# A two-block fp32 model on one core: the order of an attention, of a norm, of two PSUM banks and of a gate group changed, and three short products put into one block

## The chip, the cores and the metric

One core of one Trainium2 chip. The time is the device time of one execution in microseconds (us); times of several executions are given as their median. TensorE is called PE here (its weight loads PEld), VectorE DVE, ScalarE ACT, GpSimd POOL, SyncE SP.

## The reference, cut to what matters

The model takes 256 tokens of 1024 features through two blocks. The first has a gated short convolution, a SwiGLU feed-forward, a latent attention with 8 heads and a second SwiGLU. The second has one wide projection, a chunked band attention beside an mLSTM, a gated mix of both, and a PEER layer that chooses 16 of 16384 experts for each of 8 heads. All is float32.

```python
h = h + mla_mixer(rms_norm(h, mla_norm_g), w_dq, q_norm_g, w_uq, w_o, k_nope, k_pe, v, cos, sin)
h = h + swiglu_ffn(rms_norm(h, mla_ffn_norm_g), w13, w2)
x = rms_norm(h, final_norm_g)
h = modulate(rmsnorm(x, norm1_g), sh1, sc1)            # the "mix" norm
qa, ka, va, qkb, vb, ob, ib, fb, ga, gb = split(h @ w_in)
...
s = einsum("thpd,hpnd->thpn", q, sub_keys); s_top, i_top = top_k(s, 16)   # "the choice"
act = gelu(einsum("thkd,td->thk", u_exp[e], xb))       # here: for all experts, then gated
y = einsum("thk,thkd->td", gate * act, v_exp[e])
```

## The kernel before, in words

The kernel streams 525 blocks of weights, 128 x 1024 float32 each, through a ring of three buffers. SP loads block n into `raw` as soon as the low part of block n-3 is made. ACT rounds it to `wh` (`ahead`, line 1183, called `hi` below), DVE subtracts to get the rest `wl` (line 1736, called `lo`), and PE makes of each fp32 product three products, high x high, low x high, high x low (`three`, lines 552 to 554). A block is 24 such products of 256 columns. `hi` and `lo` run two blocks ahead of PE (LEAD = 2), and each stands at a place in the engine's program that was written by hand among that engine's other work. Each engine runs its program in order.

What the change touches, in the order of time:

- **Start.** POOL loads the condition row `cond_row`, ACT applies Silu to it (line 1277) in between the first convolution tiles, then `hi` of the next blocks.
- **Latent attention.** For each head PE makes scores (line 798), transposes probabilities (811), mixes values (820) and projects (`out_of_head`). DVE masks (2123), divides (2130, 2131), subtracts (2168), makes `lo` and a piece of the condition's product (`ada_piece`, 1905).
- **The norm "mix"** after the second feed-forward. DVE adds the eight result tiles to `h` (2003), with one `lo` after the second; ACT squares all eight tiles (1201); PE sums them over partitions (614); ACT takes the root (1215); DVE inverts and scales; ACT and DVE split into high and low parts (1225, 1779).
- **The projection** `proj(k)`, 45 blocks. Results go to the PSUM tensor `wk` of four banks; blocks 9 to 12 (vb) and 13 to 16 (va) both write banks 0 and 1 with 512 columns. ACT copies them out (1519). Beside them runs the mLSTM, unit by unit, with short PE products, DVE `m_weigh` (2303 to 2313) and ACT exponentials.
- **The choice.** `early(i)` makes the activations of 128 expert rows i; ACT writes them out (1626, 1644). During the first 77 of these blocks DVE finds the 16 best of each head and token; its `lo` calls stand there where a planner's estimated costs (`PER_LO` = 1616 per call) put them. After block 66 ACT takes an exponential (1657).
- **Gates.** Then DVE makes one-hot matrices (2552, 2556) for four tokens at a time, PE multiplies them (`gate_group`, 1092), ACT copies the result out (1631). 64 groups go with 48 further blocks, three blocks (`u_block`) to four groups; the first such trip is written out.
- `shift_phase` (line 567, 569) puts three short fp32 products, whose result nobody reads, between the products of one block: 128 columns after the second feature group, 256 after the fourth, 128 after the sixth. The kernel has it in the third block of both feed-forwards, in block 2 and block 79 of the experts' first pass and in the third block of their second pass.

The semaphores that the steps speak of: `lo_ready` (PE waits for a block's low part), `conv_kept` and `proj_act` (ACT has read a result), `probs`, `masked`, `mixed_lo` (DVE's results for the attention), `hot_ready` and `hot_used` (one-hot matrices made and used).

Of the kernel before, what the change touches and what calls it, by code (L numbers as in the profile page):

```python
# [24 lines left out]
ALU = mybir.AluOpType  # L25
# [7 lines left out]
P = 128  # L33
# [111 lines left out]
MIX_FILL = 8  # L145
DUE_AT_FIRST = -2000
# [12 lines left out]
def build(nc, stream, ada, cond, gains, consts, positions, x_in, band_bias, gate_bias, sub_keys, out, put_off):  # L159
    with ExitStack() as ctx:  # L160
# [167 lines left out]
        squares = sem("squares")  # L328
        squares_paired = sem("squares_paired")
# [126 lines left out]

        def squares_before(name):
            return sum(squares_of(m) for m, _, _ in NORMS[:NORM_NO[name]])
# [41 lines left out]
        def _(pool):  # L500
            pool.dma_start(gbias[:], gate_bias).then_inc(gate_bias_in, 16)
            pool.wait_ge(rooted, 1)
# [46 lines left out]
        def _(pe):  # L549
# [58 lines left out]
            def norm_sum(name, c):  # L608

                if c == 0:  # L610
                    wait(pe, rooted, NORM_NO[name])
                pe.wait_ge(squares, squares_before(name) + c + 1)
# [293 lines left out]
            def proj(k):  # L906
                blk = block_no(FIRST["proj"] + k)
                bank = blk[0] % RING
                if 9 <= k < 17:
                    s = (k - 9) % 4  # L910
                    ready(blk)
                    if k == 9:
                        pe.wait_ge(conv_kept, 8)
                    elif s == 0:
                        pe.wait_ge(proj_act, 1)
                    for b in range(TB):
                        for c in range(2):
                            mm = three(wk[:, b], xh[:, 2 * s + c, b * P:(b + 1) * P], xl[:, 2 * s + c, b * P:(b + 1) * P],
                                       piece(wh, blk, c * 512, c * 512 + 512), piece(wl, blk, c * 512, c * 512 + 512),
                                       s == 0 and c == 0, s == 3 and c == 1)  # L920
# [152 lines left out]
            with pe.Fori(1, CHOICE // RING) as t:  # L1073
# [22 lines left out]
            def gates_and_early(t, first_trip):  # L1096
                def u_block(k):
                    slot = (CHOICE + k) % RING
                    if first_trip:
                        early(CHOICE + k, slot, block_no(p0 + CHOICE + k), k == 2)  # L1100
                    else:
                        early(t * RING + (CHOICE + k), slot, block_no(p0 + CHOICE + k, t))

                gate_group(t * 4, 0)
                gate_group(t * 4 + 1, 1)
                u_block(0)
                gate_group(t * 4 + 2, 0)
                u_block(1)
                gate_group(t * 4 + 3, 1)
                u_block(2)  # L1110
# [66 lines left out]
        def _(sc_e):  # L1177
# [16 lines left out]
            def square(name, c, src, src_sem=None, src_base=0):  # L1194
                if c == 0:
                    wait(sc_e, normed, normed_before(name))
# [8 lines left out]
            def norm(name, src, src_sem=None, src_base=0, splits=(), first=0):  # L1205
# [285 lines left out]
            norm("mix", h, res_add, 3 * DC, splits=[(xh, 0, 0)])  # L1491

            def proj(k, load=True):
# [36 lines left out]
            for k in range(11):  # L1530
                proj(k)
# [190 lines left out]
        def _(dve):  # L1722
# [224 lines left out]
            def ffn(stage, norm_name, turn, pieces_of, late=None, beside=None):  # L1947
# [50 lines left out]
                for c in range(DC):  # L1998
# [5 lines left out]
                    if c == 1:  # L2004
                        ahead(last)
                    if late and c >= 1:
                        late(c - 1)
                if late:
                    late(DC - 1)

# [141 lines left out]
            uq_ahead(4)  # L2152
            for i in range(HEADS + 2):
                if 1 <= i < HEADS - 1:
                    latent_mask(i + 1)
                if i + 2 == HEADS:
                    divide(i + 1, 0)
                if 2 <= i <= HEADS:
                    ahead(block_no(FIRST["attn_out"] + i - 2))
                if 1 <= i < 6:  # L2160
                    ada_piece(21 + i)
                if i + 2 < HEADS:
                    divide(i + 1, 0)
                if i == 0:
                    uq_ahead(5)
# [4 lines left out]
                if i == HEADS:  # L2170
# [72 lines left out]
            norm("mix", h, splits=[(columns(modg[:, 0]), xh, xl, 0, 0)])  # L2243
            biased(2 * DC, 6 * DC)
            scaled_gain(1, "norm2")

            def proj(k):
                blk = block_no(FIRST["proj"] + k)
                ahead(blk)
# [499 lines left out]
```

## Time and profile before

| | |
|---|---|
| median of three executions | 1621.99 us (1621.66 to 1626.71) |
| the profiled execution, its own time | 1623.73 us |
| its span, first to last instruction | 1622.0 us |
| mean granted PE clock | 0.997 |
| PE / DVE / ACT busy | 98% / 82% / 54% |

A row of the timeline gives start, duration (us), engine, line, operation, output<-inputs, count of merged instructions and, in brackets, the idle time before and what ended it. PE products overlap: the distance between their starts is what they cost.

### The profile page before, as it was taken

How to read it: one execution, taken by the hardware profiler on the slowest of the kernel's cores; microseconds unless marked ns; L12 is line 12 of the kernel's file. 1: busy time of each engine (PE TensorE's matmuls, PEld its weight loads, DVE VectorE, ACT ScalarE, POOL GpSimd, SP SyncE). 2: the span in 40 equal slices, each digit the busy share in tenths (PEclk: the TensorE clock that was granted, in tenths of full speed). 3: DMA queues.
4: the chain of work that ended last, by engine and by line, in shares of the span. 5: the costliest groups of instructions: out<-in, count | busy, mean ns of one | idle time of the engine just before them, and what ended most of it. 6: DMA issues, size and time to landing. Idle time of an engine off the chain costs nothing.

```text
span 1622.0 us, 38021 instructions
## 1 busy us (share of the span) xinstructions
PE 1597.1 (98%) x13408; PEld 1562.1 (96%) x13408; DVE 1328.5 (82%) x2244; ACT 874.2 (54%) x1400; POOL 102.9 (6%) x196
## 2 busy tenths in 40 slices
PE   9999999999999999999999999999999999999998
PEld 8999999978999988989999999999999999999998
DVE  7977777978777786677779999989998788888887
ACT  5464445746444475665665555545555555555544
POOL 0000000010110000000000000000000111111110
PEclk9999999999999999999999999999999999999999
DMA  7657777455887744445547777755555777778774
GB/s 249 226 188 259 256 256 244 152 182 163 278 277 258 249 140 143 144 144 164 166 156 232 233 240 232 224 166 165 165 171 165 236 240 241 243 238 241 242 240 152
DMA packets 108667, 339.09 MB, mean 209 GB/s; under 512 B 13600, under 2 KB 29984, under 8 KB 108480
## 3 DMA queue, kind: packets, MB, share of 16 engines
q1 hardware_dynamic: 76032, 275.81, 52.3%
q0 software_dynamic: 14000, 45.24, 9.4%
q10 hardware_dynamic: 18576, 17.28, 3.1%
q8 instruction: 34, 0.56, 0.1%
q14 instruction: 25, 0.20, 0.0%
HBM read 320.31 MB, written 17.43 MB: 208 GB/s over the span
## 4 chain that ended last, share of the span: by engine, by line
PE 81%; DVE 12%; ACT 4%; issue 2%; DMA 1%; ACTq 0%; DVEq 0%; SPq 0%
PE wk L552 15%; PE wk L554 14%; PE wk L553 14%; PE acc L552 10%; PE acc L554 10%; PE acc L553 10%; DVE wl L1736 4%; PE acc L1092 4%; ACT wh L1183 1%; ACT sq L1203 1%; DMA h<-x_in 0%; DMA raw<-stream 0%; PE acc L1040 0%; PE acc L885 0%; DVE ada_w L1905 0%
## 5 line engine op out<-in xcount | busy, mean ns | idle before, releaser
L1183 ACT ACTIVATE wh<-raw 128x1024 fp32r<-128x1024 f32 x519 | 549.8, 1060 | 490.8 <-PE acc L554 237.3
L1736 DVE TENSOR_TENSOR wl<-raw,wh 128x1024 fp32r<-128x1024 f32 x519 | 634.9, 1224 | 154.5 <-ACT wh L1183 150.1
L552 PE MATMUL wk<-xh,wh 128*128 128x256 f32 x2232 | 630.8, 283 | 9.2 <-DVE wl L1736 3.5
L553 PE MATMUL wk<-xl,wh 128*128 128x256 f32 x2232 | 619.7, 278 | 0.0
L554 PE MATMUL wk<-xh,wl 128*128 128x256 f32 x2232 | 619.6, 278 | 0.0
L552 PEld LDWEIGHTS wk<-xh,wh 128*128 128x128 f32 x2232 | 421.5, 189 | 14.9 <-issue 5.1
L553 PEld LDWEIGHTS wk<-xl,wh 128*128 128x128 f32 x2232 | 420.0, 188 | 0.2
L554 PEld LDWEIGHTS wk<-xh,wl 128*128 128x128 f32 x2232 | 419.8, 188 | 0.0
L552 PE MATMUL acc<-ph,wh 128*128 128x256 f32 x1024 | 283.1, 276 | 0.0
L553 PE MATMUL acc<-pl,wh 128*128 128x256 f32 x1024 | 282.7, 276 | 0.0
L554 PE MATMUL acc<-ph,wl 128*128 128x256 f32 x1024 | 282.6, 276 | 0.0
L552 PEld LDWEIGHTS acc<-ph,wh 128*128 128x128 f32 x1024 | 192.2, 188 | 0.2 <-issue 0.2
L553 PEld LDWEIGHTS acc<-pl,wh 128*128 128x128 f32 x1024 | 192.2, 188 | 0.0
L554 PEld LDWEIGHTS acc<-ph,wl 128*128 128x128 f32 x1024 | 192.2, 188 | 0.0
L539 POOL DMA_DIRECT2D acts<-put_off x125 | 67.3, 538 | 970.2 <-DVE w L2592 964.3
L2592 DVE TENSOR_TENSOR w<-acts,gates 128x256 f32<-128x256 f32 x128 | 82.2, 642 | 29.2 <-DVE pl L2596 27.8
L1626 ACT ACTIVATE acts<-wk 128x256 f32<-128x256 f32 x128 | 49.2, 384 | 105.2 <-PE wk L554 105.2
L552 PE MATMUL acc<-hidh,wh 128*128 128x256 f32 x336 | 92.7, 276 | 0.0
L553 PE MATMUL acc<-hidl,wh 128*128 128x256 f32 x336 | 92.7, 276 | 0.0
L554 PE MATMUL acc<-hidh,wl 128*128 128x256 f32 x336 | 92.7, 276 | 0.0
L2552 DVE TENSOR_TENSOR hot<-cst,i_t 128x1024 f32<-128x1024 f32 x64 | 78.0, 1219 | 2.8 <-ACT i_t L1661 1.9
L1092 PE MATMUL acc<-hot 128*128 128x128 f32 x512 | 66.0, 277 | 2.1 <-DVE hot L2556 2.1
(371 smaller groups left out, 2174.7 us busy)
## 6 DMA issues: line engine op xcount, KB each, us to landing
raw<-stream SPq DMA_DIRECT2D x522, 512.0 KB, 4.2
ada_w<-ada POOLq DMA_DIRECT2D x48, 512.0 KB, 4.8
put_off<-acts ACTq DMA_DIRECT2D x125, 128.0 KB, 2.3
acts<-put_off POOLq DMA_DIRECT2D x125, 128.0 KB, 3.3
bias<-band_bias POOLq DMA_DIRECT2D x8, 192.0 KB, 5.0
h<-x_in SPq DMA_DIRECT2D x2, 512.0 KB, 6.4
sk<-sub_keys POOLq DMA_DIRECT2D x1, 1024.0 KB, 7.8
out<-sq SPq DMA_DIRECT2D x4, 256.0 KB, 2.2
```

The source lines that it names most:

```text
L539: pool.dma_start(acts[:, k], row).then_inc(act_back[k], 16)
L552: pe.matmul(out_ap, a_hi, b_hi, start=start, stop=False, skip_group_check=skip)
L553: pe.matmul(out_ap, a_hi, b_lo, start=False, stop=False, skip_group_check=skip)
L554: return pe.matmul(out_ap, a_lo, b_hi, start=False, stop=stop, skip_group_check=skip)
L1092: mm = pe.matmul(acc[:, 2 + par, j * P:(j + 1) * P], hot[:, par, 1, j], hot[:, par, 0, j], start=True, stop=True)
L1183: nc.scalar.activation(wh[:, blk[0] % RING], raw[:, blk[0] % RING], ACT.Copy).then_inc(hi_ready, 1)
L1203: nc.scalar.activation(sq[:, c], src[:, c], ACT.Square).then_inc(squares, 1)
L1626: nc.scalar.activation(acts[:, k], wk[:, k, 0:T], ACT.Gelu_apprx_tanh).then_inc(act_ready, 1)
L1736: v.tensor_tensor(wl[:, s], raw[:, s], wh[:, s].bitcast(F32), ALU.subtract).then_inc(lo_ready, 1)
L2552: v.tensor_tensor(hot[:, par], const("iota").unsqueeze(1).unsqueeze(1).to_broadcast([P, 2, 4, P]), columns_of(slice(0, 2)).unsqueeze(3).to ...
L2592: v.tensor_tensor(w32[:], acts[:, k], g, ALU.mult).then_inc(w_ready, 1)
```

## The change

It moves work and adds a little. Latent attention: `divide` of the next head goes ahead of `lo`, the subtraction and the condition piece. Mix norm: two of the eight squares go to DVE, the `lo` there goes behind all eight additions, and `hi` and `lo` of projection block 2 go ahead of the split and right behind it. Banks: vb uses banks 0 and 3, va banks 1 and 3, the copies out are made in two halves, and the waits fit the banks. Gates: in the first trip block 77 comes before the second gate group, and so on. Start: the condition row is loaded once the first norm's eight tiles are split, and its Silu comes before the first kept tile. Choice: lap 12 (blocks 33 to 35) is written out and block 33 gets `shift_phase`.

```diff
+SHIFT_LAP = 11
+DVE_SQUARES = 2
+VB_BANKS = slice(0, 4, 3)
+VA_BANKS = slice(1, 4, 2)
...
-            pool.wait_ge(rooted, 1)
+            pool.wait_ge(normed, DC)
             pool.dma_start(cond_row[:], cond.partition_broadcast(P)).then_inc(cond_in, 16)
...
-                    if k == 9:
-                        pe.wait_ge(conv_kept, 8)
-                    elif s == 0:
-                        pe.wait_ge(proj_act, 1)
+                    banks = VB_BANKS if k < 13 else VA_BANKS
+                    if s == 0:
+                        pe.wait_ge(conv_kept, 6 if k == 9 else 7)
                     for b in range(TB):
+                        if k == 13 and b == 1:
+                            pe.wait_ge(last_values, 1)
...
                     if 17 <= k < 20:
-                        pe.wait_ge(proj_act, 2)
+                        if bank == 2:
+                            pe.wait_ge(conv_kept, 8)
+                        else:
+                            pe.wait_ge(proj_act, 1 + bank)
...
+            with pe.Fori(1, SHIFT_LAP) as t:
+                early_lap(t)
+            for k in range(RING):
+                early(SHIFT_LAP * RING + k, k, block_no(p0 + SHIFT_LAP * RING + k), k == 0)
+            with pe.Fori(SHIFT_LAP + 1, CHOICE // RING) as t:
+                early_lap(t)
...
                 gate_group(t * 4, 0)
+                if first_trip:
+                    u_block(0)
+                    gate_group(t * 4 + 1, 1)
+                    u_block(1)
+                    gate_group(t * 4 + 2, 0)
+                    u_block(2)
+                    gate_group(t * 4 + 3, 1)
...
                 if name == "mix":
                     nc.scalar.preload_act_table(ACT.Silu)
+                    ahead(block_no(FIRST["proj"]))
...
             ahead(block_no(3))
-            keep_conv(0)
             sc_e.wait_ge(cond_in, 16)
             nc.scalar.activation(cond_row[:], cond_row[:], ACT.Silu).then_inc(csilu_ready, 1)
+            keep_conv(0)
...
-                    nc.scalar.activation(dst, wk[:, 0:2], ACT.Copy).then_inc(proj_act, 1)
+                    banks = wk[:, VB_BANKS if k == 12 else VA_BANKS]
+                    nc.scalar.activation(dst[:, 1], banks[:, 1], ACT.Copy).then_inc(last_values, 1)
+                    nc.scalar.activation(dst[:, 0], banks[:, 0], ACT.Copy).then_inc(proj_act, 1)
...
-                    if c == 1:
+                    if norm_name == "ffn2" and c == 1:
+                        for k in range(DVE_SQUARES):
+                            dve.wait_ge(res_add, added[stage] + k + 1)
+                            v.scalar_tensor_tensor(out=sq[:, k], in0=h[:, k], scalar=gsq[:, k:k + 1], in1=h[:, k],
+                                                   op0=ALU.mult, op1=ALU.mult).then_inc(mix_squared, 1)
+                    elif c == 1:
                         ahead(last)
...
+                else:
+                    ahead(last)
...
-            uq_ahead(4)
             for i in range(HEADS + 2):
                 if 1 <= i < HEADS - 1:
                     latent_mask(i + 1)
-                if i + 2 == HEADS:
+                if i + 1 < HEADS:
                     divide(i + 1, 0)
-                if 2 <= i <= HEADS:
+                if i <= 1:
+                    uq_ahead(4 + i)
+                elif i <= HEADS:
                     ahead(block_no(FIRST["attn_out"] + i - 2))
-                if 1 <= i < 6:
-                    ada_piece(21 + i)
-                if i + 2 < HEADS:
-                    divide(i + 1, 0)
-                if i == 0:
-                    uq_ahead(5)
                 if 1 <= i <= HEADS:
...
+                if 1 <= i < 6:
+                    ada_piece(21 + i)
+                elif i == HEADS:
                     ada_piece(27)
...
             norm("mix", h, splits=[(columns(modg[:, 0]), xh, xl, 0, 0)])
+            ahead(block_no(FIRST["proj"]))
```

## Rows read from the trace of the kernel before

**Rows 1.** The page: busy time and share of PE and its weight loads.
```profile
PE 1597.1 (98%) x13408; PEld 1562.1 (96%) x13408; DVE 1328.5 (82%) x2244; ACT 874.2 (54%) x1400; POOL 102.9 (6%) x196
```
**Rows 2.** Waits of PE, whole execution: us in total, times, longest.
```profile
PE wk L552 <- DVE wl L1736: 3.5, 6, 0.8
PE wk L552 <- ACT va L1519: 2.4, 1, 2.4
PE acc L1092 <- DVE hot L2556: 2.1, 2, 1.8
PE wk L614 <- ACT sq L1201: 1.4, 2, 0.8
...
PE wk L552 <- ACT vb L1519: 0.8, 1, 0.8
PE wk L798 <- DVE stat L2123: 0.7, 1, 0.7
...
PE wk L552 <- ACT u L1506: 0.6, 1, 0.6
```
**Rows 3.** Three stretches: busy us (and count) of PE, PEld, DVE, ACT, POOL, PE clock, DMA.
```profile
35.00:80.00 45.00, 45.00 (x399) 45.00 (x399) 41.73 (x76) 20.40 (x23) 1.06 (x2) 1.00 0.69 228
...
860.00:920.00 60.00, 60.00 (x532) 60.00 (x531) 56.45 (x182) 31.83 (x44) 0.00 (x0) 1.00 0.72 236
950.00:1010.00 60.00, 60.00 (x511) 60.00 (x511) 55.34 (x170) 30.74 (x43) 0.00 (x0) 1.00 0.74 234
```
**Rows 4.** Timeline of PE where block 31 of the choice begins.
```profile
929.82 0.28 PE L554 MATMUL wk<-xh,wl 128*128 128x256 f32 x1
930.16 0.38 PE L552 MATMUL wk<-xh,wh 128*128 128x256 f32 x1
```
**Rows 5.** Timeline of ACT: results of blocks 1 and 2, the second with short products.
```profile
850.29 0.39 ACT L1626 ACTIVATE acts<-wk 128x256 f32<-128x256 f32 x1 [1.07 <-PE wk L554]
...
853.97 0.38 ACT L1626 ACTIVATE acts<-wk 128x256 f32<-128x256 f32 x1 [1.77 <-PE wk L554]
```
**Rows 6.** Waits of DVE from 936 to 1058 us, the choice's slower part.
```profile
DVE wl L1736 <- ACT wh L1183: 3.4, 8, 1.3
```
**Rows 7.** Timeline of PE: the first two gate groups.
```profile
1061.82 1.16 PE L1092 MATMUL acc<-hot 128*128 128x128 f32 x8 [0.28 <-DVE hot L2556]
1064.81 1.93 PE L1092 MATMUL acc<-hot 128*128 128x128 f32 x8 [1.84 <-DVE hot L2556]
```
**Rows 8.** Timeline of DVE: first instruction of the second one-hot pair.
```profile
1062.81 1.22 DVE L2552 TENSOR_TENSOR hot<-cst,i_t 128x1024 f32<-128x1024 f32 x1
```
**Rows 9.** Two stretches at the lower PE clock.
```profile
345.00:348.00 3.00, 3.00 (x14) 2.76 (x12) 1.32 (x5) 2.59 (x7) 0.00 (x0) 0.50 0.49 175
...
1065.00:1068.40 3.40, 3.40 (x17) 3.40 (x17) 3.25 (x4) 0.60 (x1) 0.00 (x0) 0.50 0.61 200
```
**Rows 10.** Timeline of DVE around the mix norm.
```profile
570.44 1.23 DVE L1736 TENSOR_TENSOR wl<-raw,wh 128x1024 fp32r<-128x1024 f32 x1 [1.57 <-ACT wh L1183]
...
577.79 0.48 DVE L1769 SCALAR_TENSOR_TENSOR sq<-h,modg,rs 128x256 f32<-128x256 f32 x1
```
**Rows 11.** Timeline of ACT around the mix norm.
```profile
569.35 1.06 ACT L1183 ACTIVATE wh<-raw 128x1024 fp32r<-128x1024 f32 x1 [1.97 <-DMA raw<-stream]
...
572.04 2.50 ACT L1201 ACTIVATE sq<-h,gs 128x256 f32<-128x256 f32 x6 [0.83 <-DVE h L2003]
575.49 0.47 ACT L1215 ACTIVATE sd<-wk,cols 128x256 f32<-128x256 f32 x1 [0.95 <-PE wk L614]
```
**Rows 12.** Timeline of DVE: `lo` of projection block 2, behind the mix split.
```profile
585.28 1.23 DVE L1736 TENSOR_TENSOR wl<-raw,wh 128x1024 fp32r<-128x1024 f32 x1 [0.23 <-ACT wh L1183]
```
**Rows 13.** Timeline of DVE in the mLSTM, unit 3.
```profile
639.73 0.16 DVE L2303 COPY dm<-acc 128x1 f32<-128x1 f32 x1 [1.05 <-PE acc L957]
```
**Rows 14.** Timeline of DVE in the latent attention, one head.
```profile
354.96 1.23 DVE L1736 TENSOR_TENSOR wl<-raw,wh 128x1024 fp32r<-128x1024 f32 x1 [1.95 <-ACT wh L1183]
```
**Rows 15.** Timeline of ACT near the start: Silu of the condition row.
```profile
26.89 1.06 ACT L1277 ACTIVATE cond_row<-cond_row 128x1024 f32<-128x1024 f32 x1
```

More of the change, by code:

```diff
@@ L145 @@
 MIX_FILL = 8
+SHIFT_LAP = 11
+DVE_SQUARES = 2
+assert FIRST["proj"] % RING == 0
+VB_BANKS = slice(0, 4, 3)
+VA_BANKS = slice(1, 4, 2)
 DUE_AT_FIRST = -2000
@@ L328, in build @@
         squares = sem("squares")
+        mix_squared = sem("mix_squared")
+        last_values = sem("last_values")
         squares_paired = sem("squares_paired")
@@ L454, in gain, with own_squares @@
             return gv[:, GAIN[name] + k:GAIN[name] + k + 1]
+        def own_squares(name):
+            return squares_of(name) - (DVE_SQUARES if name == "mix" else 0)
         def squares_before(name):
-            return sum(squares_of(m) for m, _, _ in NORMS[:NORM_NO[name]])
+            return sum(own_squares(m) for m, _, _ in NORMS[:NORM_NO[name]])
         def group(name):
@@ L611, in norm_sum @@
                     wait(pe, rooted, NORM_NO[name])
-                pe.wait_ge(squares, squares_before(name) + c + 1)
+                if name != "mix":
+                    pe.wait_ge(squares, squares_before(name) + c + 1)
+                elif c < DVE_SQUARES:
+                    pe.wait_ge(mix_squared, c + 1)
+                else:
+                    pe.wait_ge(squares, squares_before(name) + c + 1 - DVE_SQUARES)
                 n = squares_of(name)
@@ L911, in proj @@
                     ready(blk)
-                    if k == 9:
-                        pe.wait_ge(conv_kept, 8)
-                    elif s == 0:
-                        pe.wait_ge(proj_act, 1)
+                    banks = VB_BANKS if k < 13 else VA_BANKS
+                    if s == 0:
+                        pe.wait_ge(conv_kept, 6 if k == 9 else 7)
                     for b in range(TB):
+                        if k == 13 and b == 1:
+                            pe.wait_ge(last_values, 1)
                         for c in range(2):
-                            mm = three(wk[:, b], xh[:, 2 * s + c, b * P:(b + 1) * P], xl[:, 2 * s + c, b * P:(b + 1) * P],
+                            mm = three(wk[:, banks][:, b], xh[:, 2 * s + c, b * P:(b + 1) * P], xl[:, 2 * s + c, b * P:(b + 1) * P],
                                        piece(wh, blk, c * 512, c * 512 + 512), piece(wl, blk, c * 512, c * 512 + 512),
@@ L1072, in _, with early_lap @@
                     key_scores(3)
-            with pe.Fori(1, CHOICE // RING) as t:
+            def early_lap(t):
                 for k in range(RING):
                     early(t * RING + k, k, block_no(p0 + k, t))
+            with pe.Fori(1, SHIFT_LAP) as t:
[4 more added lines that the diff above has]
+                early_lap(t)
             early(CHOICE - 2, (CHOICE - 2) % RING, block_no(p0 + CHOICE - 2))
@@ L1104, in gates_and_early @@
                 gate_group(t * 4, 0)
[L1105 to L1110, printed above, removed]
+                if first_trip:
[5 more added lines that the diff above has]
+                    gate_group(t * 4 + 3, 1)
+                else:
+                    gate_group(t * 4 + 1, 1)
+                    u_block(0)
+                    gate_group(t * 4 + 2, 0)
+                    u_block(1)
+                    gate_group(t * 4 + 3, 1)
+                    u_block(2)
             gates_and_early(0, True)
@@ L1194, in square @@
             def square(name, c, src, src_sem=None, src_base=0):
-                if c == 0:
+                if c == (DVE_SQUARES if name == "mix" else 0):
                     wait(sc_e, normed, normed_before(name))
@@ L1490, in _ @@
             ffn("ffn2", "ffn2", 1)
-            norm("mix", h, res_add, 3 * DC, splits=[(xh, 0, 0)])
+            norm("mix", h, res_add, 3 * DC, splits=[(xh, 0, 0)], first=DVE_SQUARES)
             def proj(k, load=True):
@@ L1530, in _ @@
             for k in range(11):
-                proj(k)
+                proj(k, load=k >= 1)
             sc_e.wait_ge(gates_ready, 1)
@@ L2009, in ffn @@
                     late(DC - 1)
+                else:
+                    ahead(last)
             def final_gains():
@@ L2169, in _ @@
                                     ).then_inc(mixed_lo, 1)
-                if i == HEADS:
+                if 1 <= i < 6:
+                    ada_piece(21 + i)
+                elif i == HEADS:
                     ada_piece(27)
@@ L2248, in proj @@
                 blk = block_no(FIRST["proj"] + k)
-                ahead(blk)
+                if k >= 1:
+                    ahead(blk)
                 if k == 3:
```

## The prediction

> **What bounds the kernel now.** I read the page's first part, then PE's waits over the whole execution, then the stretches by windows, then the timelines around each edit. PE is busy 98% of the span [rows 1], so there are two ways to a shorter time: fewer waits of PE, or the same products at a smaller distance. The waits of PE that the change can reach are small and spread out: 3.5 us for low parts in six places, 2.4 for the bank of va, 2.1 for one-hot matrices, 1.4 for squares, 0.8 for vb's bank, 0.7 for the mask's maximum, 0.6 for a bank that u fills [rows 2]. They sum to 11.5 us, and some of them are only what another engine is late by.
>
> The second way is less plain. A busy PE at clock 1.00 starts 532 products in 60 us in one part of the choice and 511 in another [rows 3]: 112.8 and 117.4 ns each, 2.71 and 2.82 us for a block of 24, 0.11 apart. I call these the short and the long distance. The first turns into the second at block 31, where PE waited a third of a microsecond for the block's low part [rows 4]; it stays long from there to block 75. The early convolution runs at the short one [rows 3]. Wherever the kernel has `shift_phase` (five places that I looked at), PE leaves the block at the short distance. Whether an ordinary wait leaves it short or long, I could not tell from what stands around it.
>
> **The change, part by part.** The sum is made against the profiled execution, 1623.73 us, 1.74 above the median of the runs (1621.99), and is taken down by that at the end.
>
> *Start.* Silu of the condition row (1.06 us [rows 15], with the load of its table before it) stands ahead of `hi` of later blocks, and PE's 0.8 for a low part [rows 2] follows from it. Moved behind, it frees that: −0.8. But PE ran at the long distance just before this wait and at the short one behind it (the first row of [rows 3]). Without the wait nothing is there to change it until about 82 us: 18 blocks by 0.11 = +2.0. I give the long distance 6 in 10 and take +1.1; bounds −0.9 and +1.2.
>
> *Latent attention.* Before each `lo` DVE stands idle 1.95 us for `hi` [rows 14], and the division of the next head comes after it. It goes into that idle time, so it costs nothing; if `hi` were there earlier, it would delay `lo` by its own length instead. The probabilities come earlier, and with them the waits of 0.7 [rows 2] and the smaller ones for probabilities and subtraction, about 0.5 a head in three of the heads: −1.5, bounds 0 and −3. In the same stage PE's granted clock is 0.50 for 3 us with 14 starts [rows 9]; at 0.113 us these are 1.6, so it loses 1.4. Gaps made of many short transposed products stay there, so I keep this loss; if it went, −1.4 more.
>
> *Mix norm.* DVE reaches the `lo` behind the second addition, waits 1.57 for its `hi` and computes 1.23 [rows 10]; `hi` itself had waited 1.97 for a transfer [rows 11]. All later additions stand behind it, and ACT's six squares behind them [rows 11]. With the `lo` at the end and two squares of 0.48 ([rows 10], the nearest form) in its place, additions go on 1.57 + 1.23 − 0.96 = 1.84 earlier, and ACT, with two squares fewer, is no later with the last one. The root, 0.95 after PE's sums [rows 11], moves with it. `hi` of projection block 2 costs ACT 1.06, and lies beside DVE's inversion and first scaling, which ACT waits for. Its `lo` now directly follows the split instead of coming at 585.28 [rows 12] behind other small work, so PE waits 0.6 less for it. −2.45, bounds −1 (PE's sums or the transfer late instead) and −3.5.
>
> *Banks.* With other banks the waits of 0.6, 0.8 and 2.4 [rows 2] go, 3.8 of PE. They are not worth 3.8 to the end: beside these blocks DVE and ACT run the mLSTM as one chain (stabilizer, exponentials, split, weighting), and DVE waited 1.05 for PE in it [rows 13]. Only what makes this chain earlier is kept: the 1.05, and 0.6 for copies that begin sooner: −1.65, bounds 0 and −3.8. Copies in two halves cost ACT about 0.15 more, which its idle time covers; if it were full, the chain would pay it.
>
> *Choice.* A block with short products costs 3.68 us, from block 1's result to block 2's [rows 5], against 2.82: +0.86. Then blocks 34 to 69, 36 by 0.11 = 4.0 of PE. Here DVE is next: 55.3 of 60 us busy even in the long part [rows 3], and its waits for `hi` there are 3.4 us in all [rows 6]. When PE frees blocks sooner, those waits shrink, and when they are used up PE waits for DVE. About 0.6 of the 3.4 stays (ACT's exponential after block 66 makes one `hi` late). The end of the choice therefore comes 2.8 earlier, less about 0.1 for a larger wait at block 70: −2.7. Bounds: −3.1, all of 4.0 less 0.86, and +0.9.
>
> *Gates.* PE waits 1.84 for the second group's matrices [rows 7], which DVE starts at 1062.81 [rows 8]. Block 77 (2.7) now stands in this place and hides it. Behind the wait the granted clock is 0.50, 17 starts in 3.4 us [rows 9]; at full clock these are 1.9, so 1.5 are lost, and are not if PE is not idle. Gain 3.3. What is late next: groups now come faster after one another, the pair of matrices for group 5 (2.0 of DVE) needs the buffer of group 3, which is used only after block 79, and I work out a wait of 1.35 at group 5. −2.0; bounds +0.1 (the clock falls there instead) and −3.3. The Trainium skill, page "TensorE: Matmul & The Clock Gate", section "What's actually happening", says that a clock gate driven by PE's recent activity halves the clock when it idles; the trace agrees, the clock is 0.50 behind the 1.84. By that rule a new idle time could bring the fall back at another place, which would make this term −0.5.
>
> Sum: 1.1 − 1.5 − 2.45 − 1.65 − 2.7 − 2.0 = −9.2. 1623.73 − 9.2 − 1.74 = 1612.8.
>
> **The rivals.**
> (a) *The short products bring nothing.* PE stays long behind block 33, and they only cost 0.86: −2.7 becomes +0.9, the time 1616.4. For it: the change from short to long needed only a small pause [rows 4], so perhaps the way back depends on more than short products. Against it: each of the places with them left PE short. The Trainium skill's section "Back-to-back issue gap" on the same page gives a fixed distance for isolated products, N/2.4 + 2.5, 109 ns for 256 columns, with no dependence on what came before; rows 3 show 112.8 and 117.4 at clock 1.00, so the trace speaks against it as a full account. By it block 33 could gain nothing, which is this rival's time.
> (b) *Freed PE time comes back as waits.* In banks and gates DVE has no slack: the mLSTM chain ends when it did, and group 5 waits for nearly all that group 1 no longer does. Those two terms give 0 instead of −3.65: 1616.4. For it: DVE is 92% busy in [rows 3]'s choice, and its one-hot pairs follow each other without a pause [rows 8].
> (c) *Better at both uncertain places.* The convolution stays short (−0.8 instead of +1.1) and the fall of the clock at 345 us is avoided (−1.4), with about 1.4 of the attention's bound: 1608.1.
> (d) *Slower.* A long distance gets into the experts' second pass, 125 blocks, which begins behind the gates and is carried by its own short products today. At 0.11 a block that is +13.8, and with the rest 1626.6. It decides against the change if more than 83 blocks run long that ran short (9.2 / 0.11). Against it: that pass has `shift_phase` in its third block, unchanged.
>
> **How the numbers follow.** The forecast's case 0.55, (a) 0.07, (b) 0.17, (c) 0.16, (d) 0.05. A measurement of this kernel can tell 0.3%, 4.9 us, from no change: 1617.1 is the border of faster. The forecast's case, (c), and most of (a) and (b) lie below it; (a) with (b) is 1620. Faster 0.85, same 0.11, slower 0.04. Range: from 1606 (c, with the clock and banks at their bounds) to 1619 (b with half of a); (d) and the combination of both are left out.
>
> **What the changed kernel's profile would show.** Right: in the windows of the choice after block 33 some 530 starts in 60 us, not 511; DVE's waits for `hi` there down from 3.4 to under 1; a new wait of PE at block 70 of about 0.6 and at the end of the choice. No wait for va, vb and u; DVE's wait for PE in unit 3 of the mLSTM gone. The gate's second group without a wait, clock 1.00 behind it, and a wait of 1 to 1.5 at the sixth group. The root of the mix norm 1.8 earlier beside its stage's start. Between 30 and 80 us about 383 starts in 45 us, if the start turned long. The prediction is wrong if PE's distance in the second pass of the experts differs from before, if the shift leaves PE long, or if the mLSTM's units take as long as before.

## The result, and the profile after

The changed kernel takes 1612.82 us (1611.98 to 1615.04, 5 runs), the kernel before 1623.87 (1621.66 to 1626.71, 5 runs): ratio 0.9939, 95% interval 0.9925 to 0.9952, 11 us faster. Run once more beside later experiments it gave 1613.51 against 1620.14, ratio 0.9958 (0.9945 to 0.9972), 6.6 us faster. Both intervals exclude no change; how much the change is worth depends on more than the change, as the experiments show.

The profiled execution took 1612.82, 10.9 us less than the one before. PE's line of the page and its waits, to be held against [rows 1, 2]:
```profile
PE 1588.8 (99%) x13414; PEld 1555.7 (97%) x13414; DVE 1328.8 (82%) x2246; ACT 873.6 (54%) x1400; POOL 102.6 (6%) x196
```
```profile
PE wk L562 <- DVE wl L1773: 3.3, 8, 0.7
PE wk L835 <- DVE yl L2207: 1.9, 2, 1.1
PE acc L1118 <- DVE hot L2599: 1.7, 2, 1.4
PE wk L562 <- DVE wl L1852: 1.7, 1, 1.7
```
The waits for va, vb, u and the squares of the mix norm are gone. The wait for the subtraction `yl` has grown from 0.4 to 1.9 us. The last line's 1.7 us was 0.6 before; it stands ahead of the first weight block, whose first product starts at 9.32 us instead of 9.24, so it costs 0.1. PE's busy time fell by 8.3 of the 10.9 us with six instructions more: the larger part of the gain lies in how closely products follow one another and at which clock, the smaller in idle time. That split is rough, since the ends of products are modelled.

Where the time came from is best read from the start of the same `lo` in both traces (worked out from the timelines, us after minus before):
```
block  stage behind it        after - before   of this stage
 112   convolution, ffn1          -0.48           -0.5
 128   latent attention           -2.95           -2.5
 202   ffn2, mix norm             -5.55           -2.6
 228   banks, mLSTM               -7.07           -1.5
 296   band attention, keys       -6.76           +0.3
 346   choice, blocks 27 to 77    -9.41           -2.6
 356   first gate groups         -11.02           -1.6
 525   all that is left          -10.91           +0.1
```
What the +0.3 us between blocks 228 and 296 come from, no run shows.

In the choice, the count behind block 33 (first row) is that of [rows 3]'s short part, and only from block 70 on is the distance long again (second row). A count takes in the two or three products that already run when the window opens: in the second row 101 start inside its 12 us. Read from the starts themselves, the two distances are 113.3 and 117.8 ns. At the two places where [rows 9] show clock 0.50 it is 1.00 (last two rows):
```profile
940.00:1000.00 60.00, 60.00 (x532) 60.00 (x531) 56.63 (x172) 32.31 (x45) 0.00 (x0) 1.00 0.75 240
1035.00:1047.00 12.00, 12.00 (x104) 12.00 (x103) 11.83 (x11) 6.08 (x9) 0.00 (x0) 1.00 0.77 239
...
345.00:348.00 3.00, 2.72 (x22) 2.70 (x23) 2.87 (x9) 0.89 (x3) 0.54 (x1) 1.00 0.59 178
...
1066.50:1070.00 3.50, 2.13 (x19) 1.95 (x18) 3.36 (x4) 2.41 (x5) 0.00 (x0) 1.00 0.12 40
```
DVE's waits from block 31 to block 75, against [rows 6], and the wait of PE at block 31, against [rows 4]:
```profile
DVE wl L1773 <- ACT wh L1217: 0.7, 2, 0.5
```
```profile
922.92 0.28 PE L564 MATMUL wk<-xh,wl 128*128 128x256 f32 x1
923.40 0.38 PE L562 MATMUL wk<-xh,wh 128*128 128x256 f32 x1 [0.20 <-DVE wl L1773]
```
So the pause at block 31 is there again, longer than before (473 ns from start to start instead of 340), and PE is long for two blocks, until block 33 turns it back. The gate groups, against [rows 7]: the second has no wait, the sixth waits 1.36.
```profile
1052.40 1.16 PE L1118 MATMUL acc<-hot 128*128 128x128 f32 x8 [0.30 <-DVE hot L2599]
1056.54 1.05 PE L1118 MATMUL acc<-hot 128*128 128x128 f32 x8
...
1068.06 1.16 PE L1118 MATMUL acc<-hot 128*128 128x128 f32 x8 [1.36 <-DVE hot L2599]
```
DVE's `lo` in the attention, one a head, against [rows 14]: the wait is 0.40, and the distance from head to head is 5.63 us (354.82 to 360.44). In the kernel before the row of [rows 14] belongs to the head right behind the lower clock; the two heads behind it waited 1.62 and are 6.53 apart.
```profile
361.49 1.23 DVE L1736 TENSOR_TENSOR wl<-raw,wh 128x1024 fp32r<-128x1024 f32 x1 [1.62 <-ACT wh L1183]
368.02 1.23 DVE L1736 TENSOR_TENSOR wl<-raw,wh 128x1024 fp32r<-128x1024 f32 x1 [1.62 <-ACT wh L1183]
```
The changed kernel:
```profile
349.19 1.22 DVE L1773 TENSOR_TENSOR wl<-raw,wh 128x1024 fp32r<-128x1024 f32 x1 [0.40 <-ACT wh L1217]
354.82 1.23 DVE L1773 TENSOR_TENSOR wl<-raw,wh 128x1024 fp32r<-128x1024 f32 x1 [0.40 <-ACT wh L1217]
360.44 1.23 DVE L1773 TENSOR_TENSOR wl<-raw,wh 128x1024 fp32r<-128x1024 f32 x1 [0.40 <-ACT wh L1217]
```
ACT at the mix norm, against [rows 11]: the `hi` waits 1.05 for its transfer, not 1.97, and the six squares and the root follow 4.9 us earlier by the clock of the run, of which 3.0 were gained before the stage.
```profile
565.47 1.06 ACT L1217 ACTIVATE wh<-raw 128x1024 fp32r<-128x1024 f32 x1 [1.05 <-DMA raw<-stream]
567.11 2.50 ACT L1235 ACTIVATE sq<-h,gs 128x256 f32<-128x256 f32 x6 [0.58 <-DVE h L2040]
570.65 0.47 ACT L1249 ACTIVATE sd<-wk,cols 128x256 f32<-128x256 f32 x1 [1.04 <-PE wk L629]
...
572.44 1.06 ACT L1217 ACTIVATE wh<-raw 128x1024 fp32r<-128x1024 f32 x1
```

### The profile page after: what moved, and what is told of

Its sections match the earlier page's. It is cut to its first block, busy times and chain, and to the rows that moved or that the text cites. A ratio compares the mean times of both kernels' runs of the same rounds, so it can differ in the third digit from the quotient of the medians.

```text
span 1611.1 us, 38030 instructions
## 1 busy us (share of the span) xinstructions
PE 1588.8 (99%) x13414; PEld 1555.7 (97%) x13414; DVE 1328.8 (82%) x2246; ACT 873.6 (54%) x1400; POOL 102.6 (6%) x196
## 4 chain that ended last, share of the span: by engine, by line
PE 79%; DVE 13%; ACT 4%; issue 3%; DMA 1%; ACTq 0%; POOL 0%; DVEq 0%; SPq 0%
PE wk L562 15%; PE wk L563 14%; PE wk L564 14%; PE acc L562 10%; PE acc L564 10%; PE acc L563 10%; DVE wl L1773 5%; PE acc L1118 4%; ACT wh L1217 2%; ACT sq L1237 1%; DMA h<-x_in 0%; PE acc L1059 0%; PE acc L900 0%; DVE ada_w L1942 0%; DVE sc L2164 0%
```

## The experiments

The theory: each part of the change acts where the prediction put it, and in the choice three short products turn PE from the long distance to the short one. The rivals: short products only cost, or DVE bounds the choice so that PE's pace is worth nothing.

Each interval below is of the ratio to the kernel before, run beside it. Five experiments (1 and 6 to 9) have one part of the change alone, and none of the five intervals lies below 1.0000. What they show is read from their traces, stage by stage, one execution each. The new start was never run alone.

**1. The short products alone.** The kernel before, and in it
```diff
...
+            for k in range(RING):
+                early(SHIFT_LAP * RING + k, k, block_no(p0 + SHIFT_LAP * RING + k), k == 0)
...
```


> The kernel before with nothing but short products in block 33 of the choice. Theory (short products turn PE's distance from long to short): behind block 33 PE makes 24 products in 2.72 us instead of 2.83, some 530 starts in 60 us, DVE's waits for hi from 936 to 1058 fall from 3.4 to under 1 us, and the end of the choice comes 2.5 us earlier although block 33 itself costs 0.86 more: 1621.4 against 1623.9. Rival (the short products only cost, and the gain behind block 33 in the changed kernel came from the shifted start of its stages): distance stays 117.8 ns, time 0.9 us longer, 1624.8.

Measured: 1620.56 us (11 runs) against 1622.10, ratio 0.9990 (0.9981 to 1.0000). The profiled execution is short behind block 33, and from block 296 to 346 it is 3.2 us shorter than in the trace before:
```profile
865.00:925.00 60.00, 60.00 (x532) 60.00 (x531) 56.53 (x178) 32.05 (x45) 0.00 (x0) 1.00 0.70 238
945.00:1005.00 60.00, 60.00 (x532) 60.00 (x531) 56.61 (x163) 31.98 (x45) 0.00 (x0) 1.00 0.69 240
```
But here PE was already short when block 33 began: its pause at block 31 was a mere 0.26 us from start to start, and it left the distance as it was. So this trace doesn't show the turn, and the small ratio is a first sign that the kernel before is not always long there.

**2. All but the short products.** The changed kernel with
```diff
-            with pe.Fori(1, SHIFT_LAP) as t:
-                early_lap(t)
-            for k in range(RING):
-                early(SHIFT_LAP * RING + k, k, block_no(p0 + SHIFT_LAP * RING + k), k == 0)
-            with pe.Fori(SHIFT_LAP + 1, CHOICE // RING) as t:
-                early_lap(t)
+            with pe.Fori(1, CHOICE // RING) as t:
+                for k in range(RING):
+                    early(t * RING + k, k, block_no(p0 + k, t))
```


> The changed kernel with lap 12 of the choice as before, no short products in block 33. Theory: PE waits about 0.2 us at block 31 and stays at the long distance to block 75; the end of the choice comes 2.5 us later than in the changed kernel, so 1615.3 to 1616 in all. The gates lose nothing. Rival (DVE bounds the choice alone): no more than 0.5 us either way, about 1612.8. A third way: with other arrival times the distance after block 31's wait is short by itself, then the time is 0.9 us shorter than the changed kernel's.

Measured: 1615.81 us, ratio 0.9964 (0.9950 to 0.9977). The wait at block 31 is 0.20, PE is long behind it (512 starts in 60 us), and from block 296 to 346 this trace takes 2.6 us more than the changed kernel's. This is the theory's number, and it speaks against the rival in which DVE alone bounds the choice. The medians don't tell this kernel from the changed one (0.9958, 0.9945 to 0.9972, when run again); the traces do. Here PE came long to block 33 and stayed long; in the changed kernel's first trace and in those of experiments 4 and 10 it came long and left short.
```profile
865.00:920.00 55.00, 55.00 (x488) 55.00 (x487) 51.77 (x152) 29.46 (x41) 0.00 (x0) 1.00 0.69 236
940.00:1000.00 60.00, 60.00 (x512) 60.00 (x511) 55.25 (x170) 30.57 (x43) 0.00 (x0) 1.00 0.69 236
```

**3. One short product in place of three.** In block 33 only the first one:
```diff
-                if on and c in (1, 5):
+                if on and c in ((1,) if on == "first" else (1, 5)):
...
-                elif on and c == 3:
+                elif on and on != "first" and c == 3:
...
-                early(SHIFT_LAP * RING + k, k, block_no(p0 + SHIFT_LAP * RING + k), k == 0)
+                early(SHIFT_LAP * RING + k, k, block_no(p0 + SHIFT_LAP * RING + k), k == 0 and 'first')
```


> The changed kernel, but block 33 holds only the first of its three short products (128 columns, behind the second feature group). In the changed kernel's trace the distance was short for the two feature groups after the first short product, long for the two after the second, and short again after the third. Theory (each short product turns long into short and back): one is enough, PE runs short from the third feature group of block 33 to block 69, and block 33 costs about 0.3 us instead of 0.86; since DVE is next in line, the end moves 0 to 0.5 us earlier: 1612.3 to 1612.8. Rival (three are needed, it is their sum or their time that counts): PE is long behind block 33, and the time is 2.5 us longer, 1615.3.

Measured: 1616.18 us, ratio 0.9964 (0.9951 to 0.9978). The outcome is the rival's, the reason is neither's: in this execution PE was short when block 33 began (block 31 was 495 ns, start to start, behind the product before it), and the single product turned it to long, until block 75. Whether one product is enough where PE is long, this run doesn't show at block 33; the counts at the end of this text do.

**4. One more, where PE is short.** The changed kernel with a single product of 128 columns in block 45 as well:
```diff
-            with pe.Fori(SHIFT_LAP + 1, CHOICE // RING) as t:
+            with pe.Fori(SHIFT_LAP + 1, BACK_LAP) as t:
                 early_lap(t)
+            for k in range(RING):
+                early(BACK_LAP * RING + k, k, block_no(p0 + BACK_LAP * RING + k), "first" if k == 0 else False)
+            with pe.Fori(BACK_LAP + 1, CHOICE // RING) as t:
+                early_lap(t)
```


> The changed kernel with one more short product, a single one of 128 columns in block 45, where PE runs at the short distance. Theory (a short product turns the distance over, whichever it is): from block 45 on PE runs long, some 511 starts in 60 us, DVE's waits for hi come back there (about 2 us), and the end comes 1.5 to 2.2 us later: 1614.3 to 1615. Rival (short products can only bring the short distance): nothing but their own 0.3 us, hidden or not, 1612.8 to 1613.1.

Measured: 1616.88 us, ratio 0.9972 (0.9960 to 0.9983), above the 1614.3 to 1615 expected; in the trace blocks 296 to 346 take 2.5 us more than the changed kernel's, where 1.5 to 2.2 were expected. The turn comes with the product itself. The starts around block 45's product (timeline of PE: 0.11 apart ahead of it, 0.12 behind), and 28 us on either side of it (windows):
```profile
963.39 0.28 PE L563 MATMUL wk<-xh,wh 128*128 128x256 f32 x1
963.50 0.28 PE L564 MATMUL wk<-xl,wh 128*128 128x256 f32 x1
963.62 0.28 PE L565 MATMUL wk<-xh,wl 128*128 128x256 f32 x1
963.73 0.38 PE L578 MATMUL wk<-h 128*128 128x128 f32 x2
963.87 0.36 PE L563 MATMUL wk<-xh,wh 128*128 128x256 f32 x1
964.07 0.28 PE L564 MATMUL wk<-xl,wh 128*128 128x256 f32 x1
964.19 0.28 PE L565 MATMUL wk<-xh,wl 128*128 128x256 f32 x1
964.31 0.28 PE L563 MATMUL wk<-xh,wh 128*128 128x256 f32 x1
```
```profile
934.00:962.00 28.00, 28.00 (x249) 28.00 (x248) 26.29 (x67) 14.88 (x21) 0.00 (x0) 1.00 0.69 236
966.00:994.00 28.00, 28.00 (x240) 28.00 (x240) 25.94 (x78) 14.46 (x20) 0.00 (x0) 1.00 0.67 233
```
Nothing waits here, and DVE, ACT and the weights are as they were: a product of 128 columns in the stream is cause enough, and it can do harm as well as good.

**5. Two in place of three, everywhere.**
```diff
-                if on and c in (1, 5):
+                if on and c == 5:
```


> The changed kernel without the first of the three short products (128 columns, behind the second feature group) in all its places: both feed-forwards, blocks 2, 33 and 79 of the experts' first pass, third block of the second. Theory read from five traces (a product of 128 columns turns long into short and short into long; the one of 256 columns with the constant as weights leaves long behind it, whatever was before): the last two are enough, PE leaves each such block at the short distance, and each place costs 0.23 us less (113 + 29 + 207 - 118 ns): 1.1 to 1.4 us in all, 1611.5. Rival (all three are needed): PE is long behind these places in the second pass and the feed-forwards, 0.11 us a block, over 20 us longer, 1630 and more.

Measured: 1615.40 us, ratio 0.9953 (0.9936 to 0.9970). Five of six places are left short; block 2 of the choice is left long, and PE stays long from there to block 33, whose pair turns it back. The distances of the starts around block 2's pair, in ns:
```
117 118 119 [256 columns: 215 27] 306 122 116 114 113 117 [128 columns: 108 29] 201 118 117 118 118
```
Here the product of 256 columns left the short distance behind it, and the one of 128 turned that over. Against the changed kernel it lost 2.2 us from block 272 to 312 by this, and the cheaper places (0.2 us each) don't pay for it. Another 1.2 us come from the start, which is long to 82 us in this execution. My rule that 256 columns always leave long fell in this one place of 77 in all traces.

**6. The gates alone.** The kernel before with
```diff
                 gate_group(t * 4, 0)
+                if first_trip:
+                    u_block(0)
+                    gate_group(t * 4 + 1, 1)
+                    u_block(1)
...
```


> The kernel before with nothing but the order of the first gate trip. Theory: the wait of 1.84 before the second group goes, the clock stays at 1.00 behind it, a wait of 1.35 comes before the sixth group: 2.0 us earlier from the first gate group to the experts' second pass. Rival (the wait is only passed on and the clock falls behind the sixth group): 0 to 0.5.

Measured: 1622.16 us, ratio 0.9996 (0.9983 to 1.0008). From block 346 to 356 it is 1.70 us shorter than the trace before, and the sixth group waits 1.36. But three traces with the *old* order (experiments 1, 8 and 9), each with the wait of 1.84, are 1.62, 1.53 and 1.62 shorter too. In these the clock doesn't fall. The same stretch as [rows 9]'s 17 starts, in experiment 8:
```profile
1060.30:1063.70 3.40, 3.40 (x31) 3.40 (x31) 3.25 (x4) 0.60 (x1) 0.00 (x0) 1.00 0.60 200
```
The fall comes in two of five traces with the old order, and in none of nine with the new one. So this part is worth about 0.1 us, and 1.6 in an execution in which the clock would have fallen.

**7. The banks alone.** The kernel before with
```diff
+                    banks = VB_BANKS if k < 13 else VA_BANKS
+                    if s == 0:
+                        pe.wait_ge(conv_kept, 6 if k == 9 else 7)
...
+                    nc.scalar.activation(dst[:, 1], banks[:, 1], ACT.Copy).then_inc(last_values, 1)
+                    nc.scalar.activation(dst[:, 0], banks[:, 0], ACT.Copy).then_inc(proj_act, 1)
```


> The kernel before with nothing but the banks and copies of vb and va. Theory: PE's waits of 0.6, 0.8 and 2.4 go, but the mLSTM chain on DVE and ACT sets the end of the stage: 1.4 to 1.7 us earlier behind it. Rival one: all 3.8 come out at the end. Rival two: nothing does, since DVE's units take as long as before.

Measured: 1619.63 us, ratio 0.9986 (0.9971 to 1.0001). From block 202 to 228 it is 1.9 us shorter than before (the changed kernel: 1.5). That is a little above the forecast and half of rival one's 3.8; both rivals fall. This stage too has its fall of the clock with the old banks: experiments 1 and 6 show 0.50 and are 1.7 and 1.6 us longer there than before. None of the nine traces with the new banks has it. Experiment 6:
```profile
634.50:637.50 3.00, 3.00 (x16) 3.00 (x16) 1.46 (x2) 1.35 (x3) 0.00 (x0) 0.50 0.55 175
```
And in the choice, which this kernel doesn't change, it gained 3.3 us: the pause at block 31 (301 ns, start to start) left PE short all by itself.
```profile
860.00:920.00 60.00, 60.00 (x531) 60.00 (x531) 56.50 (x179) 31.73 (x45) 0.00 (x0) 1.00 0.73 238
940.00:1000.00 60.00, 60.00 (x531) 60.00 (x531) 56.97 (x160) 31.70 (x44) 0.00 (x0) 1.00 0.79 238
```

**8. The mix norm alone.** The kernel before with
```diff
+                    if norm_name == "ffn2" and c == 1:
+                        for k in range(DVE_SQUARES):
...
+                else:
+                    ahead(last)
...
             norm("mix", h, splits=[(columns(modg[:, 0]), xh, xl, 0, 0)])
+            ahead(block_no(FIRST["proj"]))
```


> The kernel before with nothing but the mix norm's order and its two squares on DVE. Theory: root 1.85 us earlier, PE's wait for the low part of projection block 2 down from 0.8 to 0.1: 2.5 us earlier behind the norm. Since the banks of va and vb still make PE wait, up to 0.5 of it may be lost there.

Measured: 1622.35 us (1617.29 to 1626.91, 10 runs), ratio 0.9999 (0.9981 to 1.0017). From block 128 to 202 it is 2.60 us shorter than before, as in the changed kernel (2.60). Four other traces with the old norm, though, are 1.0 to 1.7 us shorter than before in the same stage: in three of them `hi` waits 0.65 to 1.01 us for its transfer, in the fourth (experiment 9) not at all, and not [rows 11]'s 1.97. Experiment 6:
```profile
568.12 1.06 ACT L1198 ACTIVATE wh<-raw 128x1024 fp32r<-128x1024 f32 x1 [0.65 <-DMA raw<-stream]
```
Against an ordinary execution this part gives about 1.3 us, and the other 1.3 was one late transfer.

**9. The attention alone.** The kernel before with
```diff
-                if i + 2 == HEADS:
+                if i + 1 < HEADS:
                     divide(i + 1, 0)
-                if 2 <= i <= HEADS:
+                if i <= 1:
+                    uq_ahead(4 + i)
+                elif i <= HEADS:
                     ahead(block_no(FIRST["attn_out"] + i - 2))
...
+                if 1 <= i < 6:
+                    ada_piece(21 + i)
```


> The kernel before with nothing but the latent attention's new order. Theory from ten traces (stage 2.5 to 3.4 us shorter in the five with the new order than in the five without, and no fall of the clock near 345 us in any of the five): 2.5 to 3.3 us earlier behind the attention, clock 1.00 there; new waits of 0.86 and about 1.05 for the subtraction yl stay. Rival (the prediction's term): 1.5, with the clock's fall staying.

Measured: 1617.99 us (12 runs), ratio 0.9988 (0.9975 to 1.0001). From block 112 to 128: 2.97 shorter than before, and no fall of the clock:
```profile
345.00:349.00 4.00, 3.90 (x31) 3.75 (x31) 3.21 (x10) 2.05 (x6) 0.54 (x1) 1.00 0.72 212
```
The clock isn't the reason: experiments 1 and 6, old order and no fall there, are just 0.17 and 0.02 shorter than before in this stage. It is DVE's period, 5.63 us a head instead of 6.53. The fall does cost something: in the three old traces that have it (before, experiments 7 and 8) the head it hits takes 7.10, 7.01 and 6.90 us from `lo` to `lo` instead of 6.53. And the stage scatters by itself: experiments 7 and 8 are 1.41 and 0.61 us longer than before there, with the same order and the same fall.

**10. The subtraction first.** In the changed kernel, `yl` ahead of `lo` at i = 1 and 7:
```diff
+                if i in (1, 7):
+                    dve.wait_ge(mixed_hi, i)
+                    v.tensor_tensor(yl[:, i - 1], wk[:, 3, 0:T], yh[:, i - 1].bitcast(F32), ALU.subtract
+                                    ).then_inc(mixed_lo, 1)
...
```


> The changed kernel with the subtraction yl ahead of lo at two heads (i = 1 and 7), where ACT's yh is ready before lo begins or as it begins. Theory (these subtractions are only late because lo stands ahead of them): waits of 0.86 and 1.08 go, lo comes 0.4 to 0.6 later and PE waits for it at one of the two heads; 0.5 to 1.5 us earlier behind the attention. Rival (lo is what PE needs next): the two waits turn into waits for lo, 0 to 0.5 us later.

Measured: 1613.80 us against the changed kernel's 1613.51 on the same chip. The wait of 0.86 is gone, a wait of 0.72 has come at 350 us and the other is 1.13 instead of 1.08. The stage is 2.39 shorter than before, the changed kernel's own two traces 2.47 and 2.99. The rival's time holds, though the new wait is for `yl` again, one head later, and not for `lo`. Moving the subtraction at these two heads moves the wait and gains nothing that these traces show.

**11. Two short products in four places, three in blocks 2 and 33.**
```diff
-                if on and c in (1, 5):
+                if on and c in ((1, 5) if on == 3 else (5,)):
```
Blocks 2 and 33 call it with 3.

> The changed kernel with all three short products in blocks 2 and 33 of the experts' first pass, and only the last two of them in the other four places. Theory (in six places with two products, five were left at the short distance, and only block 2 at the long one): 0.23 us less at each of four places, 0.9 in all, 1612 to 1613. Rival (with two it depends on what was before, so now and then a place is left long): in the second pass that costs up to 13 us in some executions, and they scatter.

Measured: 1612.10 us (1611.85 to 1613.07, 6 runs), ratio 0.9946 (0.9930 to 0.9961), beside 0.9958 (0.9945 to 0.9972) of the changed kernel: lower by 1.4 us at the median, not told apart by the intervals. All its four pairs leave PE short in the profiled execution.

**12. The changed kernel again.**


> The changed kernel once more, for comparison on the same chip and for another trace: 1612 to 1615, the distance short behind block 33 again, no stretch at clock 0.50, the start either long to 38 us or long to 82 us.

Measured: 1613.51 us (1612.08 to 1619.44, 9 runs). Its profiled execution took 1615.97, and 3.8 us of that come between blocks 356 and 405: behind the gates' 1.37 us wait PE is long in every block, trip after trip.
```profile
1090.00:1150.00 60.00, 60.00 (x520) 60.00 (x519) 54.36 (x55) 31.35 (x50) 0.00 (x0) 1.00 0.49 164
```
The changed kernel's first trace has 531 starts in this stretch. It is so until the gate groups end. The eight products of 128 columns of a gate group leave the distance as it was, short in the first trace and long in this one. None of the other thirteen traces is long here, and none of the five with the old order of the gates has this wait at the sixth group; whether the new order invites the loss, one case can't show.

Of what was expected, the time and the absence of clock 0.50 (but for the last 7 us) came true. The distance behind block 33 is short again, but PE was short ahead of it, so this trace doesn't show the turn. The start is neither long to 38 nor to 82 us: PE turns long at 35 us and short again at 38.

## Why the prediction was right

The time forecast was 1612.8 and the median is 1612.82. The agreement is partly luck: the sum of the terms was −9.2 and the profiled executions differ by 10.9; the median of before that I subtracted from was 1.9 lower than that of its five runs, which made up for it. Against the 6.6 us of the second measurement the same −9.2 would have been too much.

**Start** (+1.1 forecast, −0.5 in the trace). The long distance came as expected, but for 11 us and not for 55: a pause of 0.23 us, start to start, at 38 us turned PE back. Over all traces the new order is long to 82 us in two of eight and the old one in one of six: my 6 in 10 was too high. Nor does +1.1 follow from it: 6 in 10 of +1.2 and 4 in 10 of −0.8 are +0.4. This is the worst sized term, and it was not tested by itself.

**Attention** (−1.5; −2.5, and 2.1 to 3.4 over nine traces). The mechanism is right and the term too small: I counted 0.5 us a head in three heads, the period fell 0.9 in each of the steady heads, of which a new wait of 0.86 for `yl` at the beginning and 1.08 at the end took a part back. The clock's fall mattered less than I took it for: it is in three of five traces with the old order and in one of nine with the new one, and it costs the head that it hits 0.4 to 0.6 us (experiment 9), not the 1.4 that I worked out from the starts.

**Mix norm** (−2.45; −2.6). Right to 0.15 against the one trace, but my term of 1.57 + 1.23 − 0.96 counted a wait that belongs to one execution. [rows 11] showed that it was a transfer's; I should have asked whether that transfer is always late. With the 0.65 to 1.01 of three other traces in its place the term is 1.1 to 1.5.

**Banks** (−1.65; −1.5). PE's 3.8 us of waits gave 1.5 because DVE and ACT are next, as forecast; DVE's wait of 1.05 in unit 3 is gone. The term left out that the old banks' wait is followed by a fall of the clock in two of five traces, 1.6 us each.

**Choice** (−2.7; −2.6). The bound by DVE's waits was the right way to size it: DVE waited 3.4 there [rows 6] and waits 0.7 now, a difference of 2.7. What failed is the premise that before is always long. Of thirteen executions that came short to block 31, seven left it long and six short, with no order that I can see in the pause: 300, 310, 340 and 473 to 480 ns from start to start left it long, 261, 301, 469, 472, 481 and 495 short. What the prediction calls a wait of a third of a microsecond [rows 4] is 0.34 us from start to start, of which 0.11 is the product's own. Those which stay short without help (experiments 7 and 8) are 3.3 us faster from block 296 to 346, and those which enter block 33 short and have the three products 3.2: they cost next to nothing, since DVE is the bound. So block 33 is worth 2.6 in about every second execution.

**Gates** (−2.0; −1.6). The wait of 1.35 at the sixth group was right to 0.01. But the sum 3.3 − 1.35 mixed what is always there (1.84 + 0.28 of waits against 0.30 + 0.07 + 1.36, 0.4 in all) with what only happens when the clock falls (1.5 by [rows 9]). Of the 0.4 just 0.1 comes out as time (experiment 6). The bound of +0.1 doesn't follow from the working either: with the fall moved to the sixth group the gain is 3.3 − 1.35 − 1.5 = 0.45, and the term −0.5, as the prediction itself says further on.

**The rivals.** (a) fell (experiments 2 and 4). (b) fell for the banks; for the gates it is what happens when the clock doesn't fall. (c): the profiled execution went its way at both places, −0.5 at the start and no fall at 345 us, but that gave 2.6 us (1.6 and 1.0) of the 4.7 that it counted. (d) did not happen in the second pass, but its mechanism did in the gates (experiment 12), for 3.8 us.

**The signs.** Starts in the choice, DVE's waits, the second and the sixth gate group and unit 3 came as said. The wait at block 70 is 0.22 us, not 0.6. The root of the mix norm is 1.9 earlier beside its stage's start, against 1.8 forecast; beside the four other traces with the old norm it is 0.2 to 0.9.

## What to carry to other kernels

When a kernel's stages hang on something that an execution settles by chance, a difference between two traces is not the worth of an edit: here single terms of 1.3 to 3.3 us were one late transfer, one fall of the clock, one wait that happened to leave PE long. Look for the same stage in several executions before you size a term by one, and ask of each wait whether its cause is in the program or in that run. Size a faster engine by the waits of the next one: 4.0 us of PE's pace and 3.8 of its waits gave 2.6 and 1.5, which DVE's rows told beforehand.

## What the runs showed of the hardware that was not expected

At a granted clock of 1.00 the stream of products of 256 columns runs at 113.3 or 117.8 ns, and stays at one of them until something disturbs it. A product of 128 columns (fp32, two records), where it was the first short one of a place, turned short into long in all 29 cases and long into short in 37 of 40. The three exceptions are in the second feed-forward, six products behind a wait, where the distances (114 to 123 ns) have not settled. By their neighbours they are short: the product follows the one before it by 116 or 117 ns in them and in the 29, by 118 to 121 in the 37, and the first product of 256 columns behind it takes 200 or 201 against 206 or 207. Read so, each of the 69 turned the distance over. The three of `shift_phase` together (128, 256, 128) left PE short in all 67 places of fourteen traces, whatever was before; the last two alone in nine of ten. In the changed kernel, around block 33, in ns from start to start:
```
118 121 [128: 113 28] 207 118 114 113 113 118 [256: 216 27] 305 118 118 117 118 120 [128: 108 30] 207 118 114 113 113 114
```
A wait can do either. What the chip keeps in step here, no run shows; the state behind a wait did not follow its length. The Trainium skill, page "TensorE: Matmul & The Clock Gate", section "Back-to-back issue gap", gives one warm distance for isolated products of a size, N/2.4 + 2.5, 109 ns for 256 columns, and for streams with weight loads one figure each for 128 and 512 columns; these runs show two for 256, 113.3 and 117.8.
